# Two-layer diffusion backbone on one core: the shift of the first norm added by GpSimd instead of VectorE, in the first sweep of the input projection

## The chip, the core and the metric

The kernel runs on one core of a Trainium2 chip. The metric is the device time of one execution in microseconds (us); the figure shown for a kernel is the median of several executions. The core's engines are TensorE (PE in the profile; PEld is its weight load), VectorE (DVE), ScalarE (ACT), GpSimd (POOL) and SyncE (SP, which here issues nearly all DMAs). Each engine works through its own program in order and is held back by waits on semaphores alone.

## The reference, cut to what matters

Two layers share a stream of 1024 latent tokens and 256 context tokens of width 1024. The part that the change touches is the beginning of each layer: an RMS norm, a modulation by a scale and a shift, and the input projection, with a norm over each head and a rotary turn of the queries and keys.

```python
def modulate(x, shift, scale):
    return x * (1 + scale) + shift

h = modulate(rms_norm(x), mod[:, 0], mod[:, 1])
hc = modulate(rms_norm(ctx), cmod[0], cmod[1])
proj = h @ P["w_in"]
aq, bq, cq, gates = split_queries(proj[..., :Q_COLS], P, rope)       # norm over each head, rotary turn
ak, av, bk, bv, ck, cv = split_keys_values(proj[..., Q_COLS:], P, rope)
```

Attention in three branches, their merge and a mixture of 32 experts follow, and the whole is done twice.

## The kernel before, in words

Each layer is built of four stages, one after the other: project, attend, merge, experts. The change lies in the project stage, in `project_heads`. The 1280 tokens are ten tiles of 128 rows (NT = 10; the first eight, NL = 8, are latent tokens, the last two context tokens). The stage makes six sweeps over the tiles, one for each block of 512 columns of the weight. In sweep 0 the tiles are also made ready: each is normed, scaled and shifted, transposed by TensorE into PSUM, and split into a rounded high part and a rest (the `hT` buffer), which the later sweeps only read. A product of one tile by 512 columns takes 24 matmuls (four pieces of the weight, three passes, two blocks of 128).

Nothing but the order in which the code is written sets the order on an engine. In step s of sweep 0 it is:

- VectorE (L504 to L553): `norm(s + 2)`, which is the mean square (L488), the reciprocal (L491), the multiplication by it and by 1 + scale (L493) and the addition of the shift (L496); then `norm_lo(s + 1)` (L501), the low part of the transposed tile; in steps 3 and 5 a `split` of a piece of the next sweep's weight (L471); then the norm over the heads of tile s: the sum of squares (L528), the mean (L531), the reciprocal (L534), the product with it (L538), the product with the cosines (L548); last `heads_lo(s - 2)` (L478).
- TensorE (L628 to L655): `norm_transposes(s + 1)` (L622), which waits for the shifted tile (`h_ready`); the product of tile s (L648); `transposes(s - 2)` of the turned heads (L614).
- GpSimd (L592 to L601): `rotate(s)`, the rotary turn: two products with the sines (L577) and the addition of the part with the cosines (L584). Between steps 3 and 7 it also makes, after the rotation, one or two of the parts of the rope tables for later sweeps (L563).
- ScalarE: the squares of tile s + 2, the high part of tile s + 1, the squares of the heads of tile s (L452), the high part of tile s - 2.
- SyncE: the loads of the tiles into a ring of three buffers, the weights and the stores. In step 6 it waits until tile 7 has its shift (`h_ready`, L496) and then loads the scale and shift of the context tokens over those of the latent tokens (L299). VectorE waits for them at the beginning of `norm(8)` (L485).

The tile that is normed in step s is thus transposed in step s + 1 and multiplied in step s + 2.

Of the kernel before, what the change touches and what calls it, by code (L numbers as in the profile page):

```python
# [23 lines left out]
ALU = mybir.AluOpType  # L24
# [6 lines left out]
NT, NL = T // P, SEQ // P  # L31
# [40 lines left out]
def take_waits(eng, taken):  # L72


    eng.sem_inc(taken.sem, 1)
# [141 lines left out]
def project_heads(nc, io, scr, l, nq, st, inner, ident, hT, ahead):  # L217
# [3 lines left out]
    def sb(name, shape, dt=F32):  # L221
        return st.sb(name, shape, dt, inner)
# [16 lines left out]
    RING = 3  # L239
    rows = sb("mod_rows", [P, 2, D])  # L240
    xh = [ahead.rows[:, 3 * D:4 * D]] + [sb(f"x_tile{b}", [P, D]) for b in range(1, RING)]
# [4 lines left out]
    const_in, rows_in = st.dma("ident_loaded"), st.dma("mod_rows_loaded")  # L246
    x_in = [st.dma(f"x_loaded{b}") for b in range(RING)]
    nsq, nms, nrt, nrs, plus1, nsc, nhd, ntr, nhi, nlo = (st.event(n) for n in (
        "squares", "mean_square", "root", "rstd", "scale_plus_1", "scaled", "h_ready", "h_transposed",
        "hT_hi", "hT_lo"))  # L250
# [10 lines left out]
    taken = st.event("pool_waits_taken")  # L261
# [12 lines left out]
    def kinds(p):  # L274

        return [(0, 2, 4, 1), (2, 4, 5, 2)] if p == 4 else [(0, 8, p, p % TABLES)]

    def heads_of(p):
        return 4 if p == 4 else 8

    def where(g):

        p = max(i for i in range(SWEEPS) if first[i] <= g)
        return p, g - first[p]

    def heads(buf, h0, h1):
        return buf[:, h0 * HD:h1 * HD].rearrange("p (h d) -> p h d", d=HD)

    def table_of(slot, t, which, n):
        return table[:, slot, min(t, NL), which, :].unsqueeze(1).to_broadcast([P, n, HD])  # L290
# [3 lines left out]
    with nc.Block() as block:  # L294
# [172 lines left out]
        def _(dve):  # L467
# [13 lines left out]
            def norm(t):  # L481
                b, x = t % 2, xh[t % RING]
                if t == 0 or t == NL:
                    dve.wait_ge(rows_in.sem, rows_in.done(2 * (t // NL) + 1))
                    dve.tensor_scalar(rows[:, 1, :], rows[:, 1, :], 1.0, None, ALU.add).then_inc(plus1.sem, 1)  # L485
                    dve.wait_ge(plus1.sem, plus1.done(t // NL))
                dve.wait_ge(nsq.sem, nsq.done(t))
                dve.tensor_scalar(n_stat[:, b, 1:2], n_stat[:, b, 0:1], 1.0 / D, EPS, ALU.mult, ALU.add  # L488
                                  ).then_inc(nms.sem, 1)
                dve.wait_ge(nrt.sem, nrt.done(t))  # L490
                dve.reciprocal(n_stat[:, b, 3:4], n_stat[:, b, 2:3]).then_inc(nrs.sem, 1)  # L491
                dve.wait_ge(nrs.sem, nrs.done(t))
                dve.scalar_tensor_tensor(out=x[:, :], in0=x[:, :], scalar=n_stat[:, b, 3:4],  # L493
                                         in1=rows[:, 1, :], op0=ALU.mult, op1=ALU.mult).then_inc(nsc.sem, 1)
                dve.wait_ge(nsc.sem, nsc.done(t))
                dve.tensor_tensor(x[:, :], x[:, :], rows[:, 0, :], ALU.add).then_inc(nhd.sem, 1)  # L496

            def norm_lo(t):
                dve.wait_ge(nhi.sem, nhi.done(t))
# [2 lines left out]
                                  to[:, 0].bitcast(F32), ALU.subtract).then_inc(nlo.sem, 1)  # L502

            norm(0)  # L504
            norm(1)
            split(0, 0)
            norm_lo(0)
            for q in range(1, PIECES):
                split(0, q)
            for p in range(SWEEPS):  # L510
                for s in range(n_steps[p]):
                    g, b, t = first[p] + s, (first[p] + s) % 2, s
                    if p == 0:
                        if s + 2 < NT:
                            norm(s + 2)
                        if s + 1 < NT:
                            norm_lo(s + 1)
# [36 lines left out]
        @block.gpsimd  # L554
        def _(pool):
            TABLE_PARTS = ((0, 0, 0, HD), (1, 0, HD // 2, HD // 2), (1, HD // 2, 0, HD // 2))

            def make_table(n, part):
                which, d0, g0, w = TABLE_PARTS[part]
                if part == 0 and n >= TABLES:  # L560
                    pool.wait_ge(cs.sem, cs.done(first[n - TABLES + 1] - 1))
                    pool.wait_ge(sn.sem, sn.done(first[n - TABLES + 1] - 1))
                pool.tensor_tensor(table[:, n % TABLES, :, which, d0:d0 + w], rope[:, :, which, d0:d0 + w],  # L563
                                   gain[:, n, g0:g0 + w].unsqueeze(1).to_broadcast([P, NL + 1, w]), ALU.mult
                                   ).then_inc(tab.sem, 1)

            def rotate(g):
                (p, t), b = where(g), g % 2
                w = heads_of(p) * HD
                pool.wait_ge(y.sem, y.done(g))  # L570
                if g >= 2:
                    pool.wait_ge(tr.sem, tr.done(g - 2))
                take_waits(pool, taken)
                for h0, h1, _, slot in kinds(p):
                    for half_ in range(2):
                        src = heads(normed[b], h0, h1)[:, :, (1 - half_) * 32:(1 - half_) * 32 + 32]
                        o = pool.tensor_tensor(heads(turned[b], h0, h1)[:, :, half_ * 32:half_ * 32 + 32], src,  # L577
                                               table_of(slot, t, 1, h1 - h0)[:, :, half_ * 32:half_ * 32 + 32],
                                               ALU.mult)
                o.then_inc(sn.sem, 1)  # L580
                pool.wait_ge(sn.sem, sn.done(g))
                pool.wait_ge(cs.sem, cs.done(g))
                take_waits(pool, taken)
                pool.tensor_tensor(turned[b][:, 0:w], turned[b][:, 0:w], by_cos[b][:, 0:w], ALU.add  # L584
                                   ).then_inc(tn.sem, 1)


            TABLE_AT = {(0, 3): 1, (0, 5): 2, (1, 2): 3, (2, 2): 4, (3, 2): 5}
            pool.wait_ge(tab_in.sem, tab_in.done(1))
            for part in range(3):  # L590
                make_table(0, part)
            pool.wait_ge(tab.sem, tab.done(3 - 1))  # L592
            for p in range(VALUES):
                for s in range(n_steps[p]):
                    if p and s == 0:
                        pool.wait_ge(tab.sem, tab.done(3 * (p + 1 if p < 4 else 6) - 1))
                    rotate(first[p] + s)
                    for part in range(3):
                        if (p, s - part) in TABLE_AT:
                            if TABLE_AT[p, s - part] == 1 and part == 0:  # L600
                                pool.wait_ge(more_in.sem, more_in.done(4))  # L601
                            make_table(TABLE_AT[p, s - part], part)

# [794 lines left out]
class RestOfModulation:  # L1398
# [4 lines left out]
    RING, PER = 2, 4  # L1403
# [1331 lines left out]
```

## Time and profile before

| | us |
|---|---|
| median of 3 runs | 5008.48 (5007.08 to 5009.58) |
| the profiled execution, device time | 5003.68 |
| its span, first to last instruction | 5002.1 |
| sweep 0 of layer 0, first transposition of the norm to the end of its last product | 43.27 to 134.52 |
| sweep 0 of layer 1, the same | 2649.04 to 2740.67 |
| mean granted TensorE clock | 0.959 |

TensorE is busy 91% of the span, VectorE 66%, ScalarE 49% and GpSimd 24%. These shares are means over stages with different limits. The two sweeps that the change touches are 3.7% of the span, and the profile is to be read there. A timeline gives one engine's instructions in order, with the idle time before each and the instruction that ended it. What an instruction is worth depends on whether somebody waits for it. The page of the profile gives the number of elements of a tile as 128 x N; the list of the instructions' order gives it as 128 x heads x columns for the same instruction.

### The profile page before, as it was taken

What the parts mean: (1) busy time and instruction counts of PE and PEld (TensorE: products, weight loads), DVE (VectorE), ACT (ScalarE), POOL (GpSimd) and SP (SyncE); (2) the same over time, 40 slices, a digit from 0 to 9 for tenths busy, and PEclk for the clock granted to TensorE, in tenths of its full rate; (3) what the DMA queues carried; (4) which work ended last, traced back from release to release, by engine and by line L of the source; (5) the groups of instructions that cost most, each with busy time, mean ns of one, the idle gap of its engine ahead of it and who ended that gap; (6) DMA issues with size and microseconds to landing.
All of it is one profiled execution on the core that took longest, in us unless ns stands there. A gap on an engine that the chain in (4) does not pass through costs nothing. (4 is left out here: it accounts for less than half of the span.)

```text
span 5002.1 us, 75983 instructions
## 1 busy us (share of the span) xinstructions
PE 4544.4 (91%) x25973; PEld 3776.1 (75%) x25973; DVE 3310.6 (66%) x5272; ACT 2464.5 (49%) x3056; POOL 1192.3 (24%) x921
## 2 busy tenths in 40 slices
PE   6999998889999897999967999999999987999995
PEld 4887877777877875877745878888877866788774
DVE  6653667676776567777777626677756436877776
ACT  3223555564233315777743225655633222777774
POOL 3650004400000013333334620043000001333333
PEclk8999999999999998999988999999999998999998
DMA  5645234264554566999995635253556345999998
GB/s 188 206 120 122 65 87 104 100 185 139 209 201 168 207 210 262 397 397 397 397 357 169 199 113 117 63 124 97 136 191 217 113 167 174 388 397 397 397 397 330
DMA packets 581798, 1088.92 MB, mean 218 GB/s; under 512 B 111876, under 2 KB 265380, under 8 KB 578552
## 3 DMA queue, kind: packets, MB, share of 16 engines
q1 hardware_dynamic: 531952, 919.40, 54.8%
q0 software_dynamic: 36272, 119.42, 6.6%
q10 hardware_dynamic: 13400, 47.85, 2.4%
q8 instruction: 102, 1.67, 0.1%
q14 instruction: 72, 0.59, 0.0%
HBM read 903.12 MB, written 183.43 MB: 217 GB/s over the span
## 5 line engine op out<-in xcount | busy, mean ns | idle before, releaser
L1800 PE MATMUL merge_acc<-ahead_wide,merge_w_split 128*128 128x512 f32 (+1 forms) x2880 | 638.7, 377 | 20.5 <-DMA ahead_wide<-hT 14.9
L1800 PEld LDWEIGHTS merge_acc<-ahead_wide,merge_w_split 128*128 128x128 f32 x2880 | 505.4, 190 | 128.6 <-issue 18.7
L648 PE MATMUL project_proj_acc<-ahead_wide,project_hT 128*128 128x512 f32 x2280 | 562.1, 399 | 3.0 <-DVE ahead_wide L471 1.7
L2502 DVE TENSOR_TENSOR experts_w_gate<-experts_raw_gate,experts_w_gate 128x2048 fp32r<-128x2048 f32 x146 | 363.4, 2495 | 295.8 <-ACT experts_w_gate L2398 295.8
L648 PEld LDWEIGHTS project_proj_acc<-ahead_wide,project_hT 128*128 128x128 f32 x2280 | 426.1, 191 | 94.0 <-DVE project_hT L501 4.6
L2377 POOL TENSOR_TENSOR experts_w_down<-experts_raw_down,experts_w_down 128x2048 fp32r<-128x2048 f32 x73 | 355.9, 4876 | 512.5 <-ACT experts_w_down L2398 512.5
L2549 PE MATMUL experts_gate_acc<-experts_w_gate,experts_rowsT 128*128 128x512 f32 x1752 | 432.2, 403 | 13.2 <-DVE experts_rowsT L2507 6.9
L964 DVE TENSOR_REDUCE attend_stat<-attend_scores 128x1 f32<-128x1280 f32 (+2 forms) x288 | 305.7, 1061 | 205.9 <-PE attend_scores L865 202.2
L2563 PE MATMUL experts_result_acc<-experts_w_down,experts_hiddenT 128*128 128x512 f32 x1752 | 430.1, 401 | 12.2 <-DVE experts_w_down L2502 12.2
L2549 PE MATMUL experts_up_acc<-experts_w_up,experts_rowsT 128*128 128x512 f32 x1752 | 420.6, 395 | 0.0
L2549 PEld LDWEIGHTS experts_gate_acc<-experts_w_gate,experts_rowsT 128*128 128x128 f32 x1752 | 327.0, 190 | 101.5 <-issue 22.0
L2563 PEld LDWEIGHTS experts_result_acc<-experts_w_down,experts_hiddenT 128*128 128x128 f32 x1752 | 327.1, 190 | 86.3 <-issue 12.6
L2549 PEld LDWEIGHTS experts_up_acc<-experts_w_up,experts_rowsT 128*128 128x128 f32 x1752 | 329.2, 188 | 79.6
L2398 ACT CAST experts_w_gate<-experts_raw_gate 128x2048 fp32r<-128x2048 f32 x146 | 278.7, 1912 | 214.7 <-DMA experts_raw_gate<-in_w_exp_gate_dram 196.2
L902 ACT COPY attend_probsT<-attend_scores 128x1024 f32<-128x1024 f32 (+1 forms) x288 | 216.4, 751 | 337.2 <-PE attend_scores L832 337.2
L1268 POOL TENSOR_TENSOR ahead_rows<-ahead_rows,attend_b_stat 128x640 f32<-128x640 f32 (+1 forms) x72 | 122.3, 1699 | 885.5 <-DVE attend_b_stat L1221 885.5
L2502 DVE TENSOR_TENSOR experts_w_up<-experts_raw_up,experts_w_up 128x2048 fp32r<-128x2048 f32 x146 | 327.4, 2284 | 0.8 <-ACT experts_w_up L2398 0.8
L1809 PE MATMUL merge_acc<-merge_yT,merge_w_split 128*128 128x512 f32 (+1 forms) x1440 | 319.9, 371 | 0.0
L2398 ACT CAST experts_w_up<-experts_raw_up 128x2048 fp32r<-128x2048 f32 x146 | 278.5, 1912 | 53.2 <-DMA experts_raw_up<-in_w_exp_up_dram 53.2
L914 ACT ACTIVATE attend_probs<-attend_scores,attend_stat 128x1280 f32<-128x1280 f32 (+2 forms) x288 | 284.7, 989 | 29.5 <-DVE attend_stat L972 14.0
L1629 ACT CAST merge_w_split<-ahead_rows 128x1536 fp32r<-128x1536 f32 x120 | 177.0, 1475 | 236.4 <-DMA ahead_rows<-in_w_merge_dram 128.9
L1809 PEld LDWEIGHTS merge_acc<-merge_yT,merge_w_split 128*128 128x128 f32 x1440 | 250.7, 188 | 53.0
(257 smaller groups left out, 8298.5 us busy)
## 6 DMA issues: line engine op xcount, KB each, us to landing
experts_raw_gate<-in_w_exp_gate_dram SPq DMA_DIRECT2D x146, 1024.0 KB, 13.8
experts_raw_up<-in_w_exp_up_dram SPq DMA_DIRECT2D x146, 1024.0 KB, 12.8
experts_raw_down<-in_w_exp_down_dram SPq DMA_DIRECT2D x146, 1024.0 KB, 11.4
ahead_rows<-in_w_merge_dram SPq DMA_DIRECT2D x120, 768.0 KB, 6.4
merge_mod_w_ada<-in_w_ada_rows_dram POOLq DMA_DIRECT2D x80, 512.0 KB, 3.7
qk<-project_staged SPq DMA_DIRECT2D x74, 512.0 KB, 3.4
ye<-ahead_rows ACTq DMA_DIRECT2D x73, 512.0 KB, 6.3
attend_keys<-qk SPq DMA_DIRECT2D x96, 320.0 KB, 5.6
```

The costliest lines, as they stand in the source:

```text
L648: m = pe.matmul(acc[g % 2][:, :], hT[:, a, q * KP + k, t * P:(t + 1) * P], w_split[n % SLOTS][:, c, k, :], start=(q == 0 and i == 0 and k ...
L902: act.copy(probsT[b][:, 0:n, :], scores[b][:, 0:n * P].rearrange("p (j n) -> p j n", n=P)).then_inc(ca.sem, 1)
L914: act.activation(probs[b][:, 0:sx.n * P], scores[b][:, sx.cols], ACT.Exp, scale=SCORE_SCALE, bias=stat[:, s % 4, 1:2], accum_out=stat[:, s ...
L964: dve.tensor_reduce(stat[:, k, 0:1], scores[b][:, sx.cols], AX.X, ALU.max).then_inc(mx.sem, 1)
L1629: act.copy(w_split[b][:, 0, :, :], w_raw[b][:, :, :]).then_inc(wh.sem, 1)
L1800: m = pe.matmul(acc[:, b, 0:w], w_split[b][:, a, k, :], hT[:, x, k, 0:w], start=(i == 0 and k == 0), stop=(i == 2 and k == KD - 1))
L1809: m = pe.matmul(acc[:, 3 + b, 0:w], w_split[b][:, a, KD + k, :], yT[:, x, b * KB + k, 0:w], start=(i == 0 and k == 0), stop=(i == 2 and k ...
L2377: pool.tensor_tensor(w[DOWN][:, 1, 1, :], raw[DOWN][:, 1, :], w[DOWN][:, 0, 1, :].bitcast(F32), ALU.subtract).then_inc(w_lo_pool.sem, 1)
L2398: act.copy(w[n][:, 0, half, :], raw[n][:, half, :]).then_inc(w_hi[n].sem, 1)
L2502: dve.tensor_tensor(w[n][:, 1, half, :], raw[n][:, half, :], w[n][:, 0, half, :].bitcast(F32), ALU.subtract).then_inc(w_lo[n].sem, 1)
L2549: m = pe.matmul(acc[:, :], xT[:, a, half * (KD // 2) + k, :], w[n][:, c, half, k * EH:(k + 1) * EH], start=(half == 0 and i == 0 and k == ...
L2563: m = pe.matmul(acc_y[:, c0 * 512:(c0 + 1) * 512], hT[:, a, half * (HK // 2) + k, :], w[DOWN][:, c, half, k * D + c0 * 512:k * D + (c0 + 1 ...
```

## The change

The addition of the shift is taken from VectorE's `norm` and given to GpSimd, for all ten tiles of both layers. GpSimd adds the shift of tiles 0 and 1 before it makes its first rope table, and that of tile s + 2 in front of the rotation of tile s. The event that it signals is the same `h_ready` for which TensorE and SyncE wait.

```diff
@@ VectorE, norm(t)
                 dve.scalar_tensor_tensor(out=x[:, :], in0=x[:, :], scalar=n_stat[:, b, 3:4],
                                          in1=rows[:, 1, :], op0=ALU.mult, op1=ALU.mult).then_inc(nsc.sem, 1)
-                dve.wait_ge(nsc.sem, nsc.done(t))
-                dve.tensor_tensor(x[:, :], x[:, :], rows[:, 0, :], ALU.add).then_inc(nhd.sem, 1)
@@ GpSimd
             TABLE_AT = {(0, 3): 1, (0, 5): 2, (1, 2): 3, (2, 2): 4, (3, 2): 5}
+            def add_shift(t):
+                x = xh[t % RING]
+                if t == 0 or t == NL:
+                    pool.wait_ge(rows_in.sem, rows_in.done(2 * (t // NL) + 1))
+                pool.wait_ge(nsc.sem, nsc.done(t))
+                take_waits(pool, taken)
+                pool.tensor_tensor(x[:, :], x[:, :], rows[:, 0, :], ALU.add).then_inc(nhd.sem, 1)
+
+            add_shift(0)
+            add_shift(1)
             pool.wait_ge(tab_in.sem, tab_in.done(1))
             for part in range(3):
                 make_table(0, part)
...
                 for s in range(n_steps[p]):
                     if p and s == 0:
                         pool.wait_ge(tab.sem, tab.done(3 * (p + 1 if p < 4 else 6) - 1))
+                    if p == 0 and s + 2 < NT:
+                        add_shift(s + 2)
                     rotate(first[p] + s)
```

On VectorE, in step 1 of sweep 0 of layer 0 (the norm of tile 3, then the heads of tile 1), the order changes as follows; the lines behind the removed one are renumbered, L501 to L499 and L528 to L526:

```order
 L488 TENSOR_SCALAR project_norm_stat<-project_norm_stat 128x1
 L491 RECIPROCAL project_norm_stat<-project_norm_stat 128x1
 L493 SCALAR_TENSOR_TENSOR ahead_rows<-ahead_rows,project_norm_stat,project_mod_rows 128x1024
-L496 TENSOR_TENSOR ahead_rows<-ahead_rows,project_mod_rows 128x1024
-L501 TENSOR_TENSOR project_hT<-project_hT_acc,project_hT 128x8x128
```

One instruction of 1024 columns leaves each step; nothing else moves on VectorE.

On GpSimd, steps 2 to 4 of the same sweep before (L577 and L584 are the rotation, L563 the first part of a table):

```order
L577 TENSOR_TENSOR project_turned<-project_normed,project_rope_table 128x8x32 x2
L584 TENSOR_TENSOR project_turned<-project_turned,project_by_cos 128x512
L577 TENSOR_TENSOR project_turned<-project_normed,project_rope_table 128x8x32 x2
L584 TENSOR_TENSOR project_turned<-project_turned,project_by_cos 128x512
L563 TENSOR_TENSOR project_rope_table<-project_rope,project_gains 128x9x64
L577 TENSOR_TENSOR project_turned<-project_normed,project_rope_table 128x8x32 x2
L584 TENSOR_TENSOR project_turned<-project_turned,project_by_cos 128x512
```

and now (L593 is the addition of the shift, of tiles 4, 5 and 6; L575 and L582 are the rotation, L561 the table):

```order
L593 TENSOR_TENSOR project_x_tile<-project_x_tile,project_mod_rows 128x1024
L575 TENSOR_TENSOR project_turned<-project_normed,project_rope_table 128x8x32 x2
L582 TENSOR_TENSOR project_turned<-project_turned,project_by_cos 128x512
L593 TENSOR_TENSOR project_x_tile<-project_x_tile,project_mod_rows 128x1024
L575 TENSOR_TENSOR project_turned<-project_normed,project_rope_table 128x8x32 x2
L582 TENSOR_TENSOR project_turned<-project_turned,project_by_cos 128x512
L561 TENSOR_TENSOR project_rope_table<-project_rope,project_gains 128x9x64
L593 TENSOR_TENSOR ahead_rows<-ahead_rows,project_mod_rows 128x1024
L575 TENSOR_TENSOR project_turned<-project_normed,project_rope_table 128x8x32 x2
L582 TENSOR_TENSOR project_turned<-project_turned,project_by_cos 128x512
```

The addition for tile t stands behind the rotation of tile t - 3 and, from tile 6 on, behind the part of a table that follows that rotation.

## Rows read from the trace of the kernel before

**Rows 1.** The page: busy time, share of the span, instructions.

```profile
span 5002.1 us, 75983 instructions
```

**Rows 2.** Timeline of PE, layer 0, sweep 0: start, duration, instruction, idle before.

```profile
76.09 1.09 PE L622 MATMUL project_hT_acc<-project_ident,project_x_tile 128*128 128x128 f32 x8 [1.11 <-DVE project_x_tile L496]
77.22 5.71 PE L648 MATMUL project_proj_acc<-ahead_wide,project_hT 128*128 128x512 f32 x24
82.78 0.60 PE L614 MATMUL project_turn_acc<-project_ident,project_turned 128*128 128x128 f32 x4
84.59 1.10 PE L622 MATMUL project_hT_acc<-project_ident,project_x_tile 128*128 128x128 f32 x8 [1.22 <-DVE project_x_tile L496]
```

**Rows 3.** Timeline of DVE, layer 0, sweep 0, step 2 and the norm of tile 5.

```profile
77.09 0.67 DVE L528 TENSOR_REDUCE project_head_stat<-project_square 128x8 f32<-128x512 f32 x1
...
81.02 1.28 DVE L493 SCALAR_TENSOR_TENSOR project_x_tile<-project_x_tile,project_norm_stat,project_mod_rows 128x1024 f32<-128x1024 f32 x1
82.34 2.19 DVE L496 TENSOR_TENSOR project_x_tile<-project_x_tile,project_mod_rows 128x1024 f32<-128x1024 f32 x1
84.46 1.21 DVE L501 TENSOR_TENSOR project_hT<-project_hT_acc,project_hT 128x1024 fp32r<-128x1024 f32 x1
```

**Rows 4.** Timeline of POOL in the same steps.

```profile
79.37 1.82 POOL L577 TENSOR_TENSOR project_turned<-project_normed,project_rope_table 128x256 f32<-128x256 f32 x2 [4.42 <-DVE project_normed L538]
81.39 2.06 POOL L584 TENSOR_TENSOR project_turned<-project_turned,project_by_cos 128x512 f32<-128x512 f32 x1 [0.20 <-POOL project_turned L577]
```

**Rows 5.** Timelines of PE, ACT and DVE at the end of sweep 0, layer 0.

```profile
122.83 5.75 PE L648 MATMUL project_proj_acc<-ahead_wide,project_hT 128*128 128x512 f32 x24
...
128.78 5.74 PE L648 MATMUL project_proj_acc<-ahead_wide,project_hT 128*128 128x512 f32 x24
...
128.62 0.60 ACT L452 ACTIVATE project_square<-project_proj_acc 128x512 f32<-128x512 f32 x1 [3.41 <-PE project_proj_acc L648]
...
129.25 0.69 DVE L528 TENSOR_REDUCE project_head_stat<-project_square 128x8 f32<-128x512 f32 x1 [2.01 <-ACT project_square L452]
```

**Rows 6.** POOL: a free rotation, and by line the longer additions (ns min/median/max).

```profile
140.09 1.28 POOL L584 TENSOR_TENSOR project_turned<-project_turned,project_by_cos 128x512 f32<-128x512 f32 x1 [0.20 <-POOL project_turned L577]
...
L2377 POOL TENSOR_TENSOR experts_w_down<-experts_raw_down,experts_w_down x73: 4701/4810/5991, 1950.8 to 4948.2; 128x2048 fp32r<-128x2048 f32 x73
...
L1268 POOL TENSOR_TENSOR ahead_rows<-ahead_rows,attend_b_stat x72: 465/1853/1857, 731.3 to 3460.4; 128x640 f32<-128x640 f32 x64, 128x128 f32<-128x128 f32 x8
```

**Rows 7.** Timelines of POOL and DVE, layer 1, sweep 1: a table beside the mean.

```profile
2765.72 1.43 POOL L563 TENSOR_TENSOR project_rope_table<-project_rope,project_gains 128x576 f32<-128x576 f32 x1
...
2771.87 0.81 POOL L563 TENSOR_TENSOR project_rope_table<-project_rope,project_gains 128x288 f32<-128x288 f32 x1
...
2765.75 1.43 DVE L531 TENSOR_SCALAR project_head_stat<-project_head_stat 128x8 f32<-128x8 f32 x1
```

**Rows 8.** Timelines of DVE and PE: the beginning of sweep 0, layer 0.

```profile
41.90 1.22 DVE L496 TENSOR_TENSOR ahead_rows<-ahead_rows,project_mod_rows 128x1024 f32<-128x1024 f32 x1
...
60.28 5.74 PE L648 MATMUL project_proj_acc<-ahead_wide,project_hT 128*128 128x512 f32 x24
```

**Rows 9.** Timelines of SP, DVE and PE, layer 1: the context's rows.

```profile
2706.47 0.80 SPq L299 DMA_DIRECT2D project_mod_rows<-mod  x2
...
2713.05 1.71 DVE L485 TENSOR_SCALAR project_mod_rows<-project_mod_rows 128x1024 f32<-128x1024 f32 x1 [1.01 <-DMA project_mod_rows<-mod]
...
2718.88 1.97 PE L622 MATMUL project_hT_acc<-project_ident,project_x_tile 128*128 128x128 f32 x8 [5.05 <-DVE project_x_tile L496]
```

**Rows 10.** PE in layer 1: stretches (length, busy, clock, DMA share, GB/s), timeline.

```profile
2669.00:2673.00 4.00, 2.37 (x14) 0.99 0.00 0
2673.00:2677.00 4.00, 4.00 (x13) 0.58 0.41 131
...
2671.39 1.09 PE L622 MATMUL project_hT_acc<-project_ident,ahead_rows 128*128 128x128 f32 x8 [1.59 <-DVE ahead_rows L496]
2672.53 7.34 PE L648 MATMUL project_proj_acc<-ahead_wide,project_hT 128*128 128x512 f32 x24
```

## The prediction

> **What bounds the kernel now.** I read the profile in this order. The page gives a span of 5002.1 us [rows 1]; the change touches two stretches of some 91 us in it, the first sweep of each layer. The timeline of TensorE in such a sweep comes next. Per tile it does the transpositions of the norm (1.13 us to the start of what follows), the product (5.7 us) and the transpositions of the heads (0.35 us until the next product may start), and then it waits, 1.1 and 1.2 us in the rows shown, each time for VectorE's addition of the shift [rows 2]. From one tile to the next it is 84.59 - 76.09 = 8.50 us. Where no norm is made the same engine goes from product to product in 128.78 - 122.83 = 5.95 us without a wait [rows 5], so with the transpositions of the norm some 7.0 us per tile is what it needs: 1.5 us of each tile is VectorE's. VectorE's timeline shows it without a pause in these steps: the scaling, the shift and the low part of the next tile follow each other at once [rows 3].
>
> The timelines of VectorE and GpSimd side by side show a second thing. The multiplication by the scale runs from 81.02 to 82.30; GpSimd's addition starts at 81.39 and ends at 83.45, 2.06 us instead of the 1.28 us that it takes alone; VectorE's addition of the shift starts at 82.34 and ends at 84.53, 1.08 us after GpSimd's [rows 3, 4, 6]. So instructions of these two engines that read two operands from SBUF take turns, each for its whole length, and the later one ends 1.1 to 1.15 us after the earlier. Undisturbed the addition of the shift takes 1.22 us [rows 8]; it costs 2.1 here. The tiny mean over the heads is caught as well: it started 0.03 us after a table on GpSimd and ended with it, 1.43 us instead of some 0.17 [rows 7].
>
> **What leaves VectorE.** Ten additions in each layer, 20 in all, of 84.46 - 82.34 = 2.12 us each in the steady steps. Its own work per tile falls from 8.5 to 6.4 us, below TensorE's 7.0. If VectorE's work were all, TensorE would set the pace.
>
> **What comes to GpSimd.** Twenty additions of 1024 columns. No row has this size. Through 1.28 us for 512 columns and 4.70 us for 2048 [rows 6] a straight line gives 1.28 + 512 x 3.42 / 1536 = 2.42 us, the value I take. Half of the 2048 columns, 2.35 us, is the lower bound; the operation of 640 columns at 1.85 us, carried up in proportion, gives 1.85 x 1.6 = 2.96 us, the upper one. I choose by the first pair, since it is the same kind of addition and subtraction of two full operands. Nothing makes the removed instruction's time negative here: what could be gained is in the chain below.
>
> The Trainium skill speaks against such a move: "GPSIMD Engine Reference", Engine selection, gives elementwise work to VectorE and calls GpSimd about two times slower with two inputs. Against VectorE's undisturbed 1.22 us the trace's line agrees (2.42); against the 2.12 that the instruction costs in this place it does not, and hardly anything is lost by the move as such. The same page's section "Elementwise — side-by-side cycle accounting" has 4497 ns for an addition of 2048 columns; half of it would be an estimate of 2.25 us, and the sum below would be some 2.9 us smaller.
>
> **The chain that takes the place of VectorE.** The addition of tile t stands on GpSimd behind the rotation of tile t - 3, and that rotation needs the product of tile t - 3. So there is a loop over two tiles. From the end of product s:
> - squares on ScalarE and the hand-overs, 129.25 - 128.58: 0.67 us [rows 5];
> - from VectorE's sum of squares to the end of GpSimd's rotation, 83.45 - 77.09: 6.36 us [rows 3, 4]. It stays as long, since the multiplication by the scale still stands in the rotation's way (it starts 3.93 us after the sum, 0.37 before the rotation's last addition);
> - the addition of tile s + 3: 2.42 us, with 0.1 us to TensorE (my estimate from hand-overs of 0.04 to 0.17 us in the same timelines);
> - transpositions of the norm 1.13 us and product s + 2, 5.71 us [rows 2].
>
> The sum is 16.4 us for two tiles, 8.2 us per tile against 8.5 before. Of the 1.5 us per tile that VectorE would free, 0.3 are left. Three things then stand in this chain that were beside the path before:
> - The parts of the rope tables, 1.43 us for the first and 0.81 us for the others [rows 7], now precede the additions of tiles 6 (1.43), 7 (0.81), 8 (0.81 + 1.43) and 9 (0.81). Nobody waited for them.
> - Collisions. The split of the weight in step 3 takes SBUF just ahead of the addition of tile 5 and makes it 3.4 us long; a late addition holds up the tiny mean over the heads of the following tile, and with it its rotation.
> - The context's rows. Their load starts when tile 7 has its shift, and VectorE can use them 2713.05 - 2706.47 = 6.6 us later in layer 1 [rows 9]; in layer 0 I take 5.5 us, since there it had no wait. The shift of tile 7 now comes 1.4 us later than before, while VectorE would be ready sooner. So the wait falls wholly on VectorE in front of the norm of tile 8.
>
> At the start the shift of tile 0 comes 2.42 + 0.17 instead of 1.24 us after its scaling, and the scaling of tile 1 is caught behind it. In layer 0 most of this is hidden, for the first product waits for its last piece of weight until 56 us anyway; the second starts at 60.7 instead of 60.28 [rows 8]. In layer 1 no such wait hides it, and the second product starts 1.2 us later.
>
> **Carried forward through layer 0**, each number by the pieces above (us; the last column is the trace):
>
> | tile t | sum of squares of t - 3 | rotation and tables done | shift added | product t - 1 starts | before |
> |---|---|---|---|---|---|
> | 3 | 58.2 | 65.2 | 67.6 | 68.6 | 68.8 |
> | 4 | 67.1 | 73.4 | 75.8 | 76.8 | 77.2 |
> | 5 | 75.0 | 81.4 | 84.8 | 85.8 | 85.7 |
> | 6 | 83.2 | 91.8 | 94.2 | 95.2 | 95.3 |
> | 7 | 92.2 | 101.6 | 104.0 | 105.0 | 103.9 |
> | 8 | 101.6 | 111.3 | 115.2 | 116.2 | 114.7 |
> | 9 | 113.7 | 121.6 | 124.0 | 125.0 | 122.8 |
>
> Tile 4 as an example: product 1 ends at 66.4, 67.1 is 0.67 later, 73.4 is 6.3 after that, 75.8 is the addition, and 1.0 us further on its transpositions are through. At tile 8 the rows land at 104.0 + 5.5 = 109.5, the doubled VectorE steps and the scaling end at 112.6, and the addition follows. The last product then ends at 136.7 instead of 134.5: the sweep gains 0.4 us up to its middle and loses 2.5 behind it, +2.0. In layer 1 the same steps give +1.8.
>
> One more term. TensorE's clock in layer 1 fell to a mean of 0.58 for a stretch (between its levels of 1.2 and 2.4 GHz) right after waits of 1.6 us in a row, and product 2 took 7.34 instead of 5.7 us [rows 10]. Before, VectorE was still at work and the 1.6 us cost nothing; now a product is a link of the chain and its excess shows. The trace has a second such fall in this sweep, behind the long wait for the context's rows [rows 9], where the chain has slack anyway. I take 1.4 us for both layers.
>
> **Sum**: 2.0 + 1.8 + 1.4 = +5.2 us. Behind the sweeps TensorE goes on without waits, and all later stages wait for this one, so nothing takes the shift back. The profiled execution, 5003.7 us, would be at 5008.9; it lies 4.8 us below the median of the runs, 5008.5, and the prediction for the median is 5008.5 + 5.2 = 5013.7 us. A measurement of this kernel can tell 0.2%, 10 us, from no change.
>
> **Rivals.**
> 1. *GpSimd is the bound.* If its addition is at the upper bound, 2.96 us, each lies 0.54 us later in every link and in every mean that it catches. Carried through the same table a tenth of a microsecond costs 0.85 us per sweep, so it is 5.4 x 0.85 x 2 = +9.2 more, +14.4 in all: 5023 us, slower. It decides from about 2.7 us on. For it: the 640-column rows, and that the two additional waits of the instruction may cost; against it: two rows of plain additions lie on one line.
> 2. *TensorE sets the pace.* If the rotation did not stand in front (or the lock were not met), the steps would be 7.0 us: 7 tiles x 1.5 x 2 = -21 us, 4987 us. For it: VectorE's load does fall below TensorE's. Against it: the order on GpSimd and 6.36 us from sum to rotation are plain in the rows.
> 3. *Half of it.* The collisions fall better than in my table (the rotation slips in before the scaling, 1.1 us less per loop), and the rows land sooner: 4 us less per sweep, -3 us in all, 5005 us. That is no measurable change as well.
>
> **Chances.** The forecast 0.70, rival 3 0.13, rival 1 0.14, rival 2 0.03. The forecast's own range is 5009 to 5018. The range to hold 8 in 10 takes in rival 3 and the bound of 2.96 us: 5004 to 5023. Faster by over 0.2% 0.03, within 0.82 (the forecast with rival 3, less its tail), slower 0.15.
>
> **What would show it.** The new instruction in the timeline of GpSimd: 2.4 us alone, over 3 at tile 5. VectorE with pauses in front of the sum of squares; TensorE's waits in front of the transpositions of the norm, now ended by GpSimd, about 1.2 us per tile up to tile 6 and over 3 at tile 8; a wait of VectorE for the context's rows of 1 to 4 us in both layers; the last product of sweep 0 ending 2 us later. It would be wrong if the steady steps were under 7.6 us, if the additions took over 2.7 us, or if TensorE waited there for VectorE still.

## The result, and the profile after

The changed kernel takes 5014.22 us (median of 20 runs), the kernel before in the same comparison 5007.01 us (20 runs). The ratio is 1.0015, with a 95% interval of 1.0008 to 1.0022: slower by 7 us, less than the 10 us that were named as what can be told from no change, though the interval excludes 1. The forecast was 5013.7 us in a range of 5004 to 5023, with 0.82 on no measurable change.

The page of the changed kernel gives the longer span, 5002.1 before [rows 1]:

```profile
span 5008.2 us, 76003 instructions
```

TensorE in sweep 0 of layer 0, the same timeline as [rows 2] and [rows 8] (start, duration, instruction, idle before and its releaser):

```profile
59.88 5.73 PE L658 MATMUL project_proj_acc<-ahead_wide,project_hT 128*128 128x512 f32 x24
...
75.00 1.09 PE L632 MATMUL project_hT_acc<-project_ident,project_x_tile 128*128 128x128 f32 x8 [1.06 <-POOL project_x_tile L593]
75.85 5.74 PE L658 MATMUL project_proj_acc<-ahead_wide,project_hT 128*128 128x512 f32 x24
...
83.92 1.14 PE L632 MATMUL project_hT_acc<-project_ident,project_x_tile 128*128 128x128 f32 x8 [1.90 <-POOL project_x_tile L593]
84.77 7.30 PE L658 MATMUL project_proj_acc<-ahead_wide,project_hT 128*128 128x512 f32 x24
...
103.24 1.09 PE L632 MATMUL project_hT_acc<-project_ident,project_x_tile 128*128 128x128 f32 x8 [3.08 <-POOL project_x_tile L593]
104.09 5.73 PE L658 MATMUL project_proj_acc<-ahead_wide,project_hT 128*128 128x512 f32 x24
...
115.14 1.61 PE L632 MATMUL project_hT_acc<-project_ident,project_x_tile 128*128 128x128 f32 x8 [4.88 <-POOL project_x_tile L593]
...
124.62 5.74 PE L658 MATMUL project_proj_acc<-ahead_wide,project_hT 128*128 128x512 f32 x24
...
130.56 5.74 PE L658 MATMUL project_proj_acc<-ahead_wide,project_hT 128*128 128x512 f32 x24
```

The transpositions of the norm still wait, now for GpSimd (L593) instead of VectorE (L496 in [rows 2]), and for tiles 3 to 6 no longer in sum (4.9 us, before 6.2). At tile 7 they wait 3.08 us, where they had no wait before, and at tile 8 4.88 us, where it was 3.06:

```profile
113.07 1.97 PE L622 MATMUL project_hT_acc<-project_ident,project_x_tile 128*128 128x128 f32 x8 [3.06 <-DVE project_x_tile L496]
```

GpSimd and VectorE in the same sweep, to be laid beside [rows 3] and [rows 4]:

```profile
76.47 1.83 POOL L575 TENSOR_TENSOR project_turned<-project_normed,project_rope_table 128x256 f32<-128x256 f32 x2 [1.52 <-DVE project_normed L536]
78.50 2.06 POOL L582 TENSOR_TENSOR project_turned<-project_turned,project_by_cos 128x512 f32<-128x512 f32 x1 [0.20 <-POOL project_turned L575]
80.52 3.35 POOL L593 TENSOR_TENSOR project_x_tile<-project_x_tile,project_mod_rows 128x1024 f32<-128x1024 f32 x1
...
89.36 1.43 POOL L561 TENSOR_TENSOR project_rope_table<-project_rope,project_gains 128x576 f32<-128x576 f32 x1
90.75 2.38 POOL L593 TENSOR_TENSOR ahead_rows<-ahead_rows,project_mod_rows 128x1024 f32<-128x1024 f32 x1
```

```profile
78.12 1.28 DVE L493 SCALAR_TENSOR_TENSOR project_x_tile<-project_x_tile,project_norm_stat,project_mod_rows 128x1024 f32<-128x1024 f32 x1
79.32 1.22 DVE L499 TENSOR_TENSOR project_hT<-project_hT_acc,project_hT 128x1024 fp32r<-128x1024 f32 x1
80.45 1.21 DVE L471 TENSOR_TENSOR ahead_wide<-ahead_rows,ahead_wide 128x1024 fp32r<-128x1024 f32 x1
82.25 0.69 DVE L526 TENSOR_REDUCE project_head_stat<-project_square 128x8 f32<-128x512 f32 x1 [0.58 <-ACT project_square L452]
82.97 0.92 DVE L529 TENSOR_SCALAR project_head_stat<-project_head_stat 128x8 f32<-128x8 f32 x1
...
101.12 2.10 DVE L529 TENSOR_SCALAR project_head_stat<-project_head_stat 128x8 f32<-128x8 f32 x1
...
109.75 0.88 DVE L485 TENSOR_SCALAR project_mod_rows<-project_mod_rows 128x1024 f32<-128x1024 f32 x1 [4.00 <-DMA project_mod_rows<-mod]
```

The scaling of tile 5 ends at 79.40; the rotation's last addition, held up by it, at 80.56; the addition of the shift of tile 5 stands right behind, and since the split of the weight (L471, 80.45) came first, it takes 3.35 us. Alone it is 2.37 us, by the line of the instruction (twelve of the twenty; the other eight have a median of 2.37 too):

```profile
L593 POOL TENSOR_TENSOR project_x_tile<-project_x_tile,project_mod_rows x12: 2334/2369/3353, 44.9 to 2720.9; 128x1024 f32<-128x1024 f32 x12
```

The mean over the heads, which has 8 columns, is caught behind the additions of tiles 5 and 7, for 0.92 and 2.10 us; and at tile 8 VectorE waits 4.00 us for the context's rows (3.75 us in layer 1; before 0 and 1.01 [rows 9]).

For the comparisons below, a sweep is measured from the issue of its load of the modulation rows on SyncE to the end of its last product on TensorE. That takes in what the start costs. Two profiles of each of the two kernels give:

| us | layer 0 | layer 1 | both |
|---|---|---|---|
| before, first and second profile | 102.5, 102.0 | 103.4, 102.5 | 205.9, 204.5 |
| changed, first and second profile | 104.75, 104.9 | 104.6, 104.5 | 209.35, 209.4 |

The sweeps are 4.2 us longer by the means (205.2 and 209.4).

### The profile page after: what moved, and what is told of

Same layout as the page of the kernel before. It is cut to its first block and busy times, and to the rows that moved or that the text cites. A ratio compares the mean times of both kernels' runs of the same rounds, so it can differ in the third digit from the quotient of the medians.

```text
span 5008.2 us, 76003 instructions
## 1 busy us (share of the span) xinstructions
PE 4542.5 (91%) x25973; PEld 3778.8 (75%) x25973; DVE 3291.5 (66%) x5252; ACT 2469.0 (49%) x3056; POOL 1233.8 (25%) x941
## 5 line engine op out<-in xcount | busy, mean ns | idle before, releaser
L2512 DVE TENSOR_TENSOR experts_w_gate<-experts_raw_gate,experts_w_gate 128x2048 fp32r<-128x2048 f32 x146 | 373.7, 2569 | 282.9 <-ACT experts_w_gate L2408 282.9
```

The lines of the kernel that those rows point to most:

```text
L2512: dve.tensor_tensor(w[n][:, 1, half, :], raw[n][:, half, :], w[n][:, 0, half, :].bitcast(F32), ALU.subtract).then_inc(w_lo[n].sem, 1)
```

## The experiments

All are built from the changed kernel but the sixth and the ninth. The times are medians of 11 runs; the ratio is to the kernel before, timed beside it. The sweeps are of one profile for each run; the two profiles of the kernel before differ by 1.4 us in them, so differences of 1 to 2 us between two runs' sweeps are not told from chance.

| run | median, us | ratio (95%) | both sweeps, us |
|---|---|---|---|
| e1_tables | 5005.53 | 1.0009 (1.0000 to 1.0018) | 204.4 |
| e2_rows | 5006.39 | 1.0004 (0.9995 to 1.0013) | 209.6 |
| e3_front | 4998.42 | 0.9992 (0.9983 to 1.0001) | 201.4 |
| e4_half | 5014.84 | 1.0023 (1.0014 to 1.0032) | 196.7 |
| e5_all | 4998.55 | 0.9990 (0.9981 to 0.9999) | 195.4 |
| e6_before_tr | 5002.77 | 0.9994 (0.9985 to 1.0003) | 203.4 |
| e7_after_again | 5010.20 | 1.0012 (1.0003 to 1.0021) | 209.4 |
| e8_ahead | 5009.85 | 1.0012 (1.0003 to 1.0021) | 210.0 |
| e9_before_again | 5003.22 | 0.9998 (0.9989 to 1.0007) | 204.5 |
| e10_front_tables | 4999.55 | 0.9991 (0.9982 to 1.0000) | 196.0 |

**The tables later.**

```diff
-            TABLE_AT = {(0, 3): 1, (0, 5): 2, (1, 2): 3, (2, 2): 4, (3, 2): 5}
+            TABLE_AT = {(0, 7): 1, (1, 0): 2, (1, 3): 3, (2, 2): 4, (3, 2): 5}
```

> The changed kernel with the parts of the rope tables 1 and 2 made later (table 1 in steps 7 to 9 of sweep 0, table 2 in steps 0 to 2 of sweep 1, table 3 in steps 3 to 5), so that no table stands ahead of an addition of tiles 6 to 9 but the one of tile 9 in step 7... its first part behind the rotation of step 7, after the last addition. Theory A (a loop over two tiles: rotation, table, addition, transpositions, product): the additions of tiles 6 to 9 come earlier, products 5 to 8 start 1.5, 2, 2 and 3 us earlier; each first sweep is some 3 us shorter than in the changed kernel (about 97.9 and 97.5 us from the first doubling of the scale row to the last product), 6 us in all, so about 1 to 3 us below the kernel before. Theory B (what costs is only that GpSimd's addition is longer and takes turns with VectorE, the order on GpSimd does not matter): under 1 us against the changed kernel, still 5 to 7 us above before.

The sweeps took 204.4 us, 5.0 less than in the changed kernel where 6 was expected, though not 3 in each layer: 3.6 in layer 0 and 1.4 in layer 1, where product 2 had a slow clock (6.69 us). The addition of tile 6 now follows the rotation at once, and that of tile 7 as well, but it meets the split of a weight (L471) there and takes 3.34 us:

```profile
86.55 2.06 POOL L582 TENSOR_TENSOR project_turned<-project_turned,project_by_cos 128x512 f32<-128x512 f32 x1 [0.20 <-POOL project_turned L575]
88.57 2.37 POOL L593 TENSOR_TENSOR ahead_rows<-ahead_rows,project_mod_rows 128x1024 f32<-128x1024 f32 x1
...
96.75 3.34 POOL L593 TENSOR_TENSOR project_x_tile<-project_x_tile,project_mod_rows 128x1024 f32<-128x1024 f32 x1
```

The tables had been beside the path and the change put them into it. By the medians the kernel comes out 2.5 us above the kernel before and not below; the interval reaches from 0 to 0.18%.

**The addition in front of the rotation.**

```diff
-                    if p == 0 and s + 2 < NT:
-                        add_shift(s + 2)
+                    if p == 0 and s == 0:
+                        add_shift(2)
+                    if p == 0 and s + 3 < NT:
+                        add_shift(s + 3)
                     rotate(first[p] + s)
```

> The changed kernel with the addition of tile t in front of the rotation of tile t - 3 and no more behind it (GpSimd: add 0, 1, table, add 2, then add s + 3 and rotate s). Theory A: the rotation leaves the loop; it becomes 0.67 + 5.2 + 0.2 + 2.4 + 0.1 + 0.9 + 5.7 = 15.1 us for two tiles; the rotation has two tiles of slack before TensorE transposes it. The sweeps are 4.4 and 4.1 us shorter than in the changed kernel, 8.5 in all: 3 to 5 us below the kernel before. The rest of the gain is eaten by the wait for the context's rows at tile 8, which stays. Theory B (the addition's own length decides, not its place): under 1 us, since as many instructions of the same length run; if the rotation were needed soon, it would be slower.

8.0 us shorter sweeps, where 8.5 were expected (2.9 in layer 0 and 5.1 in layer 1, not the 4.4 and 4.1 named); the kernel is 4.6 us faster than before by the medians, with an interval that just reaches 1. GpSimd and TensorE in layer 1 of this kernel:

```profile
2674.04 2.38 POOL L593 TENSOR_TENSOR project_x_tile<-project_x_tile,project_mod_rows 128x1024 f32<-128x1024 f32 x1 [2.57 <-DVE project_x_tile L493]
2676.37 1.43 POOL L575 TENSOR_TENSOR project_turned<-project_normed,project_rope_table 128x256 f32<-128x256 f32 x2
2678.00 1.29 POOL L582 TENSOR_TENSOR project_turned<-project_turned,project_by_cos 128x512 f32<-128x512 f32 x1 [0.20 <-POOL project_turned L575]
```

```profile
2669.49 5.73 PE L660 MATMUL project_proj_acc<-ahead_wide,project_hT 128*128 128x512 f32 x24
...
2677.33 5.72 PE L660 MATMUL project_proj_acc<-ahead_wide,project_hT 128*128 128x512 f32 x24
```

GpSimd now waits for the scaling alone, the rotation follows with no harm (its last addition is 1.29 us again), and nobody waits for it. As many instructions of the same length run on GpSimd as in the changed kernel: theory B, that only their length counts, has fallen. VectorE's wait for the context's rows is nearly gone as well, 0.36 us in layer 0 and 0.58 in layer 1 instead of 4.00 and 3.75, though its load was not touched:

```profile
107.46 0.69 DVE L485 TENSOR_SCALAR project_mod_rows<-project_mod_rows 128x1024 f32<-128x1024 f32 x1 [0.36 <-DMA project_mod_rows<-mod]
```

**Half of the addition.** The tensor operation of `add_shift` on 512 columns; the other half gets no shift.

> The changed kernel with an addition of 512 of the 1024 columns alone (the shift of the other half is left out): GpSimd's addition is 1.28 us instead of 2.36. Theory A: each of its places in the loop is 1.08 us shorter, carried forward with the collisions the two sweeps lose 7.2 and 7.8 us, 15 us in all, to 9 to 11 us below the kernel before; that is 0.7 us per sweep for a tenth of a microsecond. If the addition were beside the path (the loss from the context's rows or from elsewhere in the kernel alone), the sweeps would change by under 2 us each.

The sweeps took 99.5 and 97.2 us, 5.3 and 7.4 less than in the changed kernel (7.2 and 7.8 expected), so 1.1 us of each addition (2.37 us whole, 1.27 half) is worth some 6.3 us per sweep: in effect the addition is on the path some six times in ten. The median says nothing here: the program executes 76269 instructions instead of 76003. The reason is most likely that with other values in the tiles the experts' routing is another one, which no run here shows.

**The context's scale row earlier.** Each row has its own semaphore, the scale row is asked for first at the start of the sweep too, and in step 6 SyncE does:

```diff
-                            sp.wait_ge(nhd.sem, nhd.done(NL - 1))
-                            load_rows(1)
+                            sp.wait_ge(nsc.sem, nsc.done(NL - 1))
+                            load_row(1, 1)
+                            sp.wait_ge(nhd.sem, nhd.done(NL - 1))
+                            load_row(1, 0)
```

> The changed kernel with the context's scale row loaded over the old one as soon as tile 7 is scaled (by VectorE), and only the shift row after its addition (by GpSimd), each with its own semaphore. Theory A: VectorE's wait for the rows at tile 8 (4.0 and 3.75 us in the changed kernel) goes; the addition of tile 8 then waits for the shift row or for the tables in front of it, so of the 4 us some 2 us per sweep are seen: the sweeps about 1.8 and 2.6 us shorter than in the changed kernel, 4.4 us in all, which leaves 1 to 3 us above the kernel before. Theory B: the wait of VectorE is covered by TensorE's own and nothing changes (under 1 us).

A miss by the sweeps of its profile, for which 4.4 us less were expected. VectorE's wait is gone, and yet they are no shorter (209.6; 1.9 longer in layer 0, 1.6 shorter in layer 1):

```profile
108.95 0.68 DVE L487 TENSOR_SCALAR project_mod_rows<-project_mod_rows 128x1024 f32<-128x1024 f32 x1
```

```profile
112.69 2.16 POOL L563 TENSOR_TENSOR project_rope_table<-project_rope,project_gains 128x576 f32<-128x576 f32 x2
114.80 2.36 POOL L595 TENSOR_TENSOR project_x_tile<-project_x_tile,project_mod_rows 128x1024 f32<-128x1024 f32 x1
```

```profile
61.28 7.32 PE L660 MATMUL project_proj_acc<-ahead_wide,project_hT 128*128 128x512 f32 x24
...
79.05 7.12 PE L660 MATMUL project_proj_acc<-ahead_wide,project_hT 128*128 128x512 f32 x24
...
118.83 7.68 PE L660 MATMUL project_proj_acc<-ahead_wide,project_hT 128*128 128x512 f32 x24
```

The addition of tile 8 now stands behind two parts of tables (it follows the addition of tile 7 by 8.3 us from end to start, by 9.6 in the changed kernel), and three products ran at a lowered clock, each with 1.4 to 2.0 us over the usual 5.73; in the changed kernel it was two behind the first, at 84.77 and 116.39. The two effects have about the same size, and the run doesn't separate them. The granted clock is shown by stretches of 4 us (length, busy, clock, DMA share, GB/s), the first with a product at full clock, the second with the one at 79.05:

```profile
71.00:75.00 4.00, 4.00 (x20) 1.00 0.28 107
...
79.00:83.00 4.00, 4.00 (x13) 0.62 0.39 111
```

The medians don't fit these sweeps: the kernel is 3.3 us above the kernel before here and 6.3 and 7.2 us in the two comparisons of the changed kernel, which is what theory A had for it (1 to 3 us above). The intervals overlap, so neither reading is shown by this run alone.

**The three edits together.**

> The changed kernel with the three edits together: the addition of tile t in front of the rotation of tile t - 3, tables 1 and 2 made later, the context's scale row loaded as soon as tile 7 is scaled. Theory A (the loop over two tiles, tables and context's rows in it): the edits hit different links, so they add up: each first sweep 6.3 to 7.3 us shorter than in the kernel before, 13.6 us in all; one slow product by TensorE's clock at a sensitive tile in one of the sweeps takes 1.6 back. The kernel is 10 to 14 us faster than before (ratio about 0.9976). Theory B (a saving here is taken back by something else, such as the clock or TensorE's own work): not better than the third experiment alone, -4 us.

The sweeps are 9.8 us shorter than before (by the mean of its two profiles), with 13.6 expected: the edits add up, but to less than the sum. The whole kernel is 5.4 us faster, 0.10%, hardly more than with the order alone. In the sweep in layer 0 two products behind the first have a lowered clock (76.31, 7.21 us; 94.64, 6.63 us), and the additions wait for the scaling. The sweeps are 6.0 us shorter than in the third run, but the medians, each against its own kernel before, only 0.8 us better; so the timed gain of the other two edits is not told from nothing.

**The order and the tables, without the separate row.**

> The changed kernel with the addition in front of the rotation and tables 1 and 2 later, without the separate load of the context's scale row. Theory A: in the fifth experiment the additions came 2.5 us earlier in the steps before tile 8, and the separate load hides the wait for the context's rows; without it VectorE waits at tile 8 again, so the two sweeps take 198 to 199 us together against 195.4 in the fifth and 205.9 before; the kernel is 3 to 8 us faster than before. If the separate load was worth nothing (as in the second experiment, where a slow clock at three products hid what it brought), the sweeps take 195 to 196 us.

196.0 us, where theory A had 198 to 199: by the expectation's own measure the separate load is worth nothing, or 0.6 us. VectorE waits 0.56 us for the rows here, not 4, and in layer 1 not at all:

```profile
105.29 0.69 DVE L485 TENSOR_SCALAR project_mod_rows<-project_mod_rows 128x1024 f32<-128x1024 f32 x1 [0.56 <-DMA project_mod_rows<-mod]
```

With the addition in front, tile 7 has its shift earlier, and the load is nearly in time. Moving the tables alone does not do that (the wait is 3.89 us in the first run), the order alone does (0.36 us in the third). So the wait at tile 8 was a consequence of the place of the addition of tile 7, behind the rotation, rather than a cost of its own.

**Tables and row on the kernel before.**

> The kernel before (VectorE adds the shift) with two of these edits: tables 1 and 2 later, the context's scale row loaded as soon as tile 7 is scaled. Theory A: with VectorE setting the pace the tables were beside the path, and the rows cost something in layer 1 alone (1.0 us of wait and the collisions behind it): 0 us in layer 0, -2 us in layer 1. Theory B (these two edits are worth as much on the kernel before): -7 us or more.

203.4 us against a mean of 205.2: -1.8 us, +0.4 in layer 0 and -2.3 in layer 1. On VectorE's path the two edits bring little, as expected; they do not explain what the experiments on the changed kernel gained.

**One tile further ahead.** On top of the three edits, `norm(s + 3)` in the place of `norm(s + 2)` on VectorE and ScalarE, `norm(2)` before the loop.

> The fifth experiment, and VectorE and ScalarE norm one tile further ahead: norm of tile s + 3 in front of the heads of tile s. Theory A: the addition no longer waits for the heads of tile t - 3, so in the steady steps TensorE alone sets the pace, 7.0 us per tile (the products of tiles 6 to 8 follow each other in 6.9 to 7.1 us); but the norm of tile 3 then stands in front of the heads of tile 0, and the context's rows are asked for a tile earlier, which costs 2 us at the start and 2 us at tile 8: 5 us less per sweep than in the kernel before, -10 us in all, no better than the fifth.

A miss by some 15 us: the sweeps take 210.0, 14.6 more than with the three edits alone, where 10 us less than in the kernel before were expected, 195.2. The pace of TensorE is reached in single steps only: in layer 0 from product 2 to 3 and from 7 to 8 it is 6.8 us, but 7.5 from 3 to 4, 8.9 from 4 to 5 and 8.9 from 6 to 7. The loss is at the start (product 1 takes 7.83 us there, with its clock lowered) and above all at tile 8:

```profile
105.62 0.69 DVE L488 TENSOR_SCALAR project_mod_rows<-project_mod_rows 128x1024 f32<-128x1024 f32 x1 [7.61 <-DMA project_mod_rows<-mod]
```

The norm of tile 8 stands one step earlier, in front of the low part of tile 6 for which product 6 waits (9.16 us idle on TensorE), while the load stands on SyncE behind a store (98.05) and is issued at 99.11 only. I had put 2 us on it; from product 5 to product 6 it is 16.3 us, against 7.7 in the fifth run.

**Both kernels once more.**

> The changed kernel itself, beside the others of this call on one chip. By the sweeps of its profile (2.6 and 1.8 us longer than before) +4.5 us; by the first comparison +7.5 (0.15%, 0.08 to 0.22). If the sweeps are all of it, this comparison should come out nearer to +4.5; if something behind the sweeps is also slower, at +7 again.

> The kernel before, against itself, with a second profile. The comparison should hold 1.0 in its interval and say how wide a difference of nothing is. From the issue of the first sweep's load of the modulation rows to the end of its last product the two sweeps should again take 102.5 and 103.4 us (205.9 together; the changed kernel 209.3 and 209.4 in its two profiles). If the stretch from the last projection product to the first product of the merge in layer 1 is again 640.1 us (the changed kernel: 643.0 and 642.5), something behind the sweeps is slower in the changed kernel as well; if it is 641 to 643, that part of the difference between the profiles is chance.

The changed kernel came out 6.3 us above before, nearer to the 7 than to the 4.5, the kernel before 1.2 us below itself. The sweeps repeat within 1.4 us. In the second profile of the kernel before the stretch from the last projection product to the first product of the merge in layer 1 is 642.3 us instead of 640.1, as in the changed kernel (643.0 and 642.5), and its span was 5008.3 us although its sweeps were 1.4 us shorter. So a difference of some us between two single profiles behind the sweeps can be chance.

Set side by side, the four profiles still put what is longer outside the sweeps into one stretch. From the end of sweep 0 to the last projection product nothing is lost: 290.1 to 290.2 us in layer 0 in all four, in layer 1 255.5 us in both of the changed kernel, 255.4 and 258.9 in those of before. From there to the first product of the merge, the attend stage, the changed kernel takes 752.2 and 752.6 us in layer 0 against 750.9 and 750.6, and in layer 1 643.0 and 642.5 against 640.1 and 642.3: 3.2 us for both layers by the means. The change touches nothing there. With the same instructions the variants take 749.4 to 751.7 and 640.2 to 643.7 us there, and not in the order of their sweeps. So the place is known and a cause is not; two profiles each don't tell it from chance.

## Why the prediction was right

- *The mechanism.* VectorE's work fell below TensorE's and TensorE did not get the 1.5 us per tile, since the addition stands behind the rotation of tile t - 3: right. The third experiment shows it, with the same instructions in another order.
- *The pace.* From product 2 to product 3 it is 75.85 - 67.76 = 8.1 us, with 8.2 forecast; from product 1 to product 3, two tiles, 15.97 us for 16.4. Of the loop's terms squares and hand-overs (0.66), sum to rotation (6.36), addition (2.36) and product (5.74) came as forecast. The transpositions took 0.85 us up to the product, not 1.13. The 1.13 of the kernel before was misread: there the product waited for the low part on VectorE, whose instruction ends at 85.67 [rows 3], and product 4 starts at 85.72. TensorE alone thus needs 6.8 us per tile, not 7.0, as the eighth run shows in two steps. The table of steps was worked out with 1.0 us from the addition to the product in place of the 1.23 of the list, and so came closer than the sum of 16.4.
- *The addition's price.* 2.42 us taken, 2.37 measured (bounds 2.35 and 2.96); 3.35 at tile 5 for 3.4 forecast.
- *The table of steps.* Products 2, 3, 4, 5, 6, 7 and 8 start at 67.8, 75.9, 84.8, 94.0, 104.1, 116.4 and 124.6; forecast 68.6, 76.8, 85.8, 95.2, 105.0, 116.2 and 125.0. The last one ends at 136.3 for 136.7 (2.2 us after the 134.5 of before, where the sum took 2.0). In the second profile it ends at 137.0.
- *The tables*: shown on the path, 5.0 us for the two sweeps together.
- *The context's rows.* The wait is there (4.00 and 3.75 us). In layer 0 VectorE can use the rows 109.75 - 103.22 = 6.5 us after the load is issued, where 5.5 was taken. What the wait costs was sized wrongly: its cure alone brought nothing that the sweeps show, and the third and the tenth run show it to be an effect of the late tile 7. In the sum this did not matter, since the wait was in the table with the rest.
- *The clock.* Mis-sized. Product 4 ran 1.6 us long on the path (84.77, 7.30 us, mean granted clock 0.76 over it and 1.00 over product 3), and 1.4 us in layer 1: 3.0 us, and 2.3 us in the second profile, where the forecast had 1.4 us for the two layers together. Before, product 5 was slow in layer 0 and VectorE covered it.
- *The sum.* +5.2 was forecast; the sweeps show +4.2 (2.6 in layer 0 and 1.6 in layer 1), the two timed comparisons +7.2 and +6.3. Without the slow product 4 the sweeps would be some 1.2 to 1.9 us longer, for the 3.8 us of the table: one term was too small and the rest too large. The 2 to 3 us between the sweeps and the timed difference had no term in the forecast. They lie within the intervals of both ratios, and the profiles place them in the attend stage without showing a cause. It stays open.
- *Luck.* The median lies 0.5 us from the forecast because two errors cancel: the difference came out at 7.2 us and not 5.2, and the kernel before at 5007.0 us and not at the 5008.5 that the forecast was counted from. Within the sweeps the clock's term and the table's miss in opposite directions. What was right is the mechanism and the order of size.
- *Rivals.* GpSimd as the bound by an addition of 2.96 us: fallen, 2.37. TensorE setting the pace: not here. Half of the cost, by luckier collisions and rows that land sooner: the rows landed later than taken, and the loop has 6.36 us from sum to rotation as forecast.

## What to carry to other kernels

Before an instruction is handed to an idle engine, write down what stands in front of it in that engine's order, and what that waits for: here the share of busy time of GpSimd was 24%, and it was the rotation of an earlier tile, not the work, that held the shift back. If the moved instruction is wanted sooner than its neighbours, it has to go in front of them; that one edit turned some +7 us into -4.6 (an interval from -8.5 to +0.5 us). What was free behind a slow engine (tables, a load, a slow clock) gets a price once the new path runs through it.

## What the runs showed of the hardware

- VectorE and GpSimd take turns, each for its whole instruction, so an engine here is held back by more than its semaphores. Caught on VectorE were the instructions with both operands in SBUF (L471, L493, L496) and the tensor-scalar ones (L485, L529); with 1024 columns and two operands they end some 1.1 us after the other. Not caught were those with an operand in PSUM: L499 takes 1.22 us at 79.32 while GpSimd's addition runs from 78.50 to 80.56. The Trainium skill has it as an exclusive lock ("SBUF — State Buffer", Who interferes with whom), and the trace agrees. I had not expected how much a tiny instruction can lose: the mean over 8 columns took 2.10 us instead of 0.17 at 101.12, behind an addition that started at 100.85.
- TensorE's granted clock was lowered at one to three products behind the first of each such sweep, and each time the product took 0.5 to 2.9 us more than 5.73. The waits in front were 1.4 to 9.2 us long, but the wait alone doesn't decide: in layer 1 of the changed kernel product 6 took 5.74 us after a wait of 3.08 us in one profile and 7.33 us after 3.11 in the other. In the kernel before it was product 2 in layer 1 in one profile (7.34 us) and product 5 in the other (7.32 us). Which product it hits changes with the order of the other engines and between two executions, and so whether it is covered: it moves a sweep by some 2 us without any edit to TensorE's program.
